# The last MLP chunk: the squared norm is applied to the hidden tiles instead of the down tiles

## The chip, the cores and the metric

The kernel runs on one core of one Trainium2 chip. What counts is the device time of one execution, in microseconds (us), as the median of several runs.

## What is computed

A two-layer block, followed by a second block of another kind, on 512 tokens of width 1024, all in float32. Only the MLP of the first block matters here; it stands at the end of each of the two layers:

```
u = rmsnorm(x, norm_mlp[l])
x = x + jnp.square(jax.nn.relu(u @ w_mlp_up[l])) @ w_mlp_down[l]
```

`rmsnorm` multiplies each token by r = 1 / sqrt(mean of squares + eps) and each column by a gain. Since r is one positive number for a token, relu(r z)^2 = r^2 relu(z)^2. The kernel computes the up product without r and applies r^2 later; `rms` holds r^2 in every partition by then. Where it is applied is free: to the hidden tile, or to the result of the down product.

## The kernel before

Tensors lie with their features in the 128 partitions and the 512 tokens along them. Every float32 product is made of three: a value is split into a high part (`a_hi`, `b_hi`, `w_hi`, written by ScalarE) and a low part (`a_lo`, `b_lo`, by VectorE; `w_lo`, by GpSimd), and TensorE adds high x high, low x high and high x low. Weights come in blocks of 1 MB: SyncE loads block n into one of two slots (L476) when the low parts of block n-2 are done, and, for some, its sums; ScalarE makes the high part (`w_split`, or `column_high` for half a block), GpSimd the low part in four pieces.

The 4096 hidden features of the MLP are worked through in 4 chunks of 8 tiles. In a chunk, four up blocks (b = 0 to 3, two tiles each) make the hidden tiles, and four down blocks add their product to the 8 tiles of x, n = 8 to 15. In chunks 1 to 3 the up blocks are computed with fewer multiplications (`fast_block` on TensorE, seven parts in four PSUM banks), for which VectorE prepares sums of weights (`weight_sums`, `sum_low`) and puts the results together (`first_sums`, `middle_sums`, `last_sums`). The orders are written out by hand for each engine; each engine runs its queue strictly in order, with semaphores between them:

- ScalarE, `fast_ups`, for each block b: the high part of one half of the next weights, the copy of the first partial product, `late_parts` (high parts of the weight sums), raw copies for the block after, then it waits for `ups_made`, takes relu of both tiles in place (L1388), and for each tile the square into `g` (L1394, signals `h_ready`) and the same square as high part into `b_hi` (L1395, signals `h_hi`). After that it goes on with block b + 1. For b = 3 the first thing is the split of the first down block (L1132).
- VectorE, `chunk`, for each block b: `weight_sums` for block b + 1, the low parts of the two hidden tiles of block b - 1 (`h_low`: `b_lo = g - b_hi`), `first_sums` (frees PSUM bank 1), `sum_low`, `middle_sums` (bank 2), `sum_low`, `last_sums` (bank 3), and it signals `ups_made`. All their element-wise instructions go through the helper `tt`, line L1689; they are told apart by their tiles.
- For each down tile n VectorE waits for TensorE and runs `x_add`: the product by `rms` in PSUM, a drain, the addition to x. In the last chunk it then signals `x_ready`; ScalarE takes x's high part and square for the next layer, VectorE the low part and the running sums of squares (`squares`, L1768).
- At the end of layer 1 TensorE begins the second block with `plain_pair`; before its fourth step it sums the squares over the partitions (`entry_sums`, L846, 16 matmuls of one column), and waits for VectorE's sums first.

Of the kernel before, what the change touches and what calls it, by code (L numbers as in the profile page):

```python
# [8 lines left out]
ALU = mybir.AluOpType  # L9
ACT = mybir.ActivationFunctionType  # L10
# [15 lines left out]
CHUNKS = 4  # L26
# [36 lines left out]
UP = 4  # L63
# [84 lines left out]
def two_blocks(nc, weights, ada, c_rows, consts, rope, tri_bias, mult_bias, tri_mask, layer_params, params, x_in, selectors, out):  # L148
    with ExitStack() as ctx:
# [92 lines left out]
        def sem(name):  # L242
            return ctx.enter_context(nc.semaphore(name))
# [116 lines left out]
        stored = sem("stored")  # L360
        ups_made = sem("ups_made")
        relu_made = sem("relu_made")
        t_near = sem("t_near")
        t_used = sem("t_used")
        t_raw = sem("t_raw")
# [762 lines left out]
        def _(act):  # L1128
# [167 lines left out]
            for L in range(LAYERS):  # L1296
# [70 lines left out]
                def fast_ups(c):  # L1367

                    at = B_MLP + 8 * c
                    for b in range(UP):  # L1370
                        k_ = UP * (c - 1) + b
                        if b + 1 < UP:
                            column_high(at + b + 1, 0).then_inc(w_hi_ready, 1)
                        else:
                            w_split(L, at + UP)
                        if k_ == 0:
                            act.wait_ge(t_split, nth(L, 4, 3))
                        p1_copy_out(L, MLP, k_)
                        if b + 1 < UP:
                            late_parts(L, MLP, k_ + 1, at + b + 1)  # L1380
                        act.wait_ge(tile_done, nth(L, LAYER_TILES, c * 16 + first_tile(B_MLP) + 2 * b + 1))
                        if b == 0:
                            ada_load_at(c, 1)
                        if b + 2 < UP:
                            raw_copies(L, k_ + 2, at + b + 2)
                        act.wait_ge(ups_made, fast_nth(L, k_, 1, 1))
                        for u in range(2):
                            nc.scalar.activation(result[MLP][u], result[MLP][u], ACT.Relu, scale=(1.0, -1.0)[u])  # L1388
                        act.drain()
                        for u in range(2):  # L1390
                            m = 2 * b + u
                            if b > 0:
                                act.wait_ge(h_split, nth(L, 8 * CHUNKS, c * 8 + m - 2))
                            nc.scalar.activation(g[:, 6 + u, :], result[MLP][u], ACT.Square).then_inc(h_ready, 1)  # L1394
                            nc.scalar.activation(b_hi[:, m, :], result[MLP][u], ACT.Square).then_inc(h_hi, 1)  # L1395
                        if b == UP - 1:
                            w_split(L, at + UP + 1)

# [288 lines left out]
        def _(dve):  # L1687
# [315 lines left out]
            with dve.Fori(0, LAYERS) as L:  # L2003
# [39 lines left out]
                def chunk(c):  # L2043
# [25 lines left out]
                    def h_low(n):  # L2069
# [2 lines left out]
                        tt(b_lo[:, n, :], g[:, 6 + n % 2, :], f32(b_hi[:, n, :]), ALU.subtract).then_inc(h_split, 1)  # L2072
                        dve.drain()

                    def t_forms(n):

                        t1, t2, t3, t4 = (m[:, n, :] for m in x_sums_f32[MLP])
                        near, far = g[:, n % 2, :], ps[4 + n % 2]
                        dve.wait_ge(t_near, nth(L, HK, n))
                        tt(t1, near[:, 0:HS], near[:, HS:S], ALU.subtract)  # L2080
                        dve.drain()
                        nc.vector.scalar_tensor_tensor(t2, far[:, HS:S], -1.0, t1, ALU.mult, ALU.subtract)
                        tt(t3, far[:, HS:S], near[:, HS:S], ALU.subtract)
                        dve.drain()
                        nc.vector.scalar_tensor_tensor(t4, far[:, 0:HS], -1.0, t2, ALU.mult, ALU.subtract
                                                       ).then_inc(t_used, 1)
                        if n == HK - 1:
                            dve.drain().then_inc(t_raw, 4)
# [18 lines left out]
                    else:  # L2107
                        for b in range(UP):
                            k_ = UP * (c - 1) + b
                            more = b + 1 < UP  # L2110
                            if more:
                                weight_sums(L, MLP, k_ + 1, at + b + 1)
                            if b > 0:
                                for u in range(2):
                                    h_low(2 * b - 2 + u)
                            first_sums(L, MLP, k_)
                            if more:
                                sum_low(L, MLP, k_ + 1, 1)
                            middle_sums(L, MLP, k_)
                            if more:  # L2120
                                sum_low(L, MLP, k_ + 1, 2)
                            last_sums(L, MLP, first + 2 * b)
                            dve.drain().then_inc(ups_made, 1)
                        for u in range(2):
                            h_low(2 * UP - 2 + u)
                    if last_chunk:
                        modulation_gain(0)
                        dve.drain()
# [5 lines left out]
                    for n in range(8, 16):  # L2134
                        if last_chunk and n == 15:
                            squares(L, n - 9, 2 * KT + n - 9, True)
                        dve.wait_ge(tile_done, nth(L, LAYER_TILES, first + n))
                        x_add(n, n - 8, last_chunk, True)
                        if last_chunk and 8 < n < 15:
                            low_next(n - 9)  # L2140
                        if last_chunk and n == 15:
# [499 lines left out]
```

## Time and profile before

| | before |
|---|---|
| median of 3 runs (lowest, highest) | 2045.96 us (2044.22, 2046.25) |
| the profiled execution, its time | 2045.99 us |
| its span, first to last instruction | 2044.1 us |
| busy in the span: TensorE | 2034.3 us (100%) |
| VectorE | 1228.3 us (60%) |
| ScalarE | 886.3 us (43%) |
| GpSimd | 1025.8 us (50%) |
| mean granted clock of TensorE | 0.999 |

The profile names engines PE (TensorE), DVE (VectorE), ACT (ScalarE), POOL (GpSimd) and SP (SyncE). A row of the timeline gives the start in us, the length in us, engine, line, operation, written tile <- read tiles, and in brackets the idle time of the engine before it with what ended it. Instructions of one engine overlap a little, so the step between two starts is shorter than their length. The last chunk of layer 0 lies at 625 to 709 us: the up blocks start at 625.4, 635.5, 645.6 and 655.6, the down tiles at 665.7. The last chunk of layer 1 lies 702.05 us later, with the same rows.

### The profile page before, as it was taken

Reading aid. Unit: us, or ns where it says so; the run is one execution under the profiler, and the core shown is the slowest. Engines: PE = TensorE matmul, PEld = TensorE weight load, DVE = VectorE, ACT = ScalarE, POOL = GpSimd, SP = SyncE. Lnnn points to the kernel's source line nnn. Section 1 sums busy time; section 2 is a strip of 40 time slices with the busy share of each in tenths; the row PEclk is TensorE's granted clock in tenths of the full one; section 3 lists DMA queues with packets and bytes.
Section 4 is the critical chain, followed back from the end, with each engine's and each line's share of the span. In section 5 each row is a group of like instructions: output and inputs, shape, how many; then the busy total and the mean of one; then the engine's idle time right before and its main releaser. Section 6 shows DMA issues by size and latency. Waiting matters only on the chain.

```text
span 2044.1 us, 29815 instructions
## 1 busy us (share of the span) xinstructions
PE 2034.3 (100%) x10920; PEld 1715.2 (84%) x10920; DVE 1228.3 (60%) x2166; ACT 886.3 (43%) x1353; POOL 1025.8 (50%) x761
## 2 busy tenths in 40 slices
PE   9999999999999999999999999999999999999999
PEld 7788778889889878877788899898877777889898
DVE  5677335576757737854356767668445478737363
ACT  4124353536345422244445455364356544535352
POOL 5454334576555554443355765554343334556555
PEclk9999999999999999999999999999999999999999
DMA  6222212343443232221233443422222112222223
GB/s 215 98 98 89 83 63 102 115 165 107 183 151 118 104 118 97 103 83 69 77 114 124 146 148 143 170 97 103 98 83 78 67 42 96 91 103 104 104 103 104
DMA packets 36083, 222.60 MB, mean 109 GB/s; under 512 B 5308, under 2 KB 5692, under 8 KB 10336
## 3 DMA queue, kind: packets, MB, share of 16 engines
q1 hardware_dynamic: 28608, 190.66, 26.5%
q10 hardware_dynamic: 7328, 30.00, 4.3%
q8 instruction: 91, 1.49, 0.3%
q14 instruction: 56, 0.46, 0.1%
HBM read 215.65 MB, written 2.10 MB: 107 GB/s over the span
## 4 chain that ended last, share of the span: by engine, by line
PE 95%; DVE 3%; DVEq 1%; issue 0%; ACT 0%; DMA 0%; ACTq 0%; POOL 0%
PE ps L554 18%; PE ps L556 17%; PE ps L555 17%; PE ps L718 6%; PE ps L720 6%; PE ps L719 6%; PE ps L571 3%; PE ps L572 3%; PE ps L573 3%; PE ps L634 2%; PE ps L603 1%; PE ps L605 1%; PE ps L604 1%; PE ps L655 1%; PE ps L644 1%
## 5 line engine op out<-in xcount | busy, mean ns | idle before, releaser
L487 POOL TENSOR_TENSOR w_lo<-w_raw,w_hi 128x512 fp32r<-128x512 f32 x544 | 737.6, 1387 | 800.6 <-ACT w_hi L1132 790.8
L1132 ACT ACTIVATE w_hi<-w_raw 128x2048 fp32r<-128x2048 f32 x134 | 256.1, 1911 | 388.9 <-PE ps L556 289.4
L554 PE MATMUL ps<-a_hi,w_hi 128*128 128x512 f32 (+1 forms) x888 | 351.8, 396 | 0.0
L556 PE MATMUL ps<-a_hi,w_lo 128*128 128x512 f32 (+1 forms) x888 | 346.2, 390 | 0.0
L555 PE MATMUL ps<-a_lo,w_hi 128*128 128x512 f32 (+1 forms) x888 | 345.8, 389 | 0.0
L501 POOL TENSOR_TENSOR w_lo<-w_raw,w_hi 128x512 fp32r<-128x512 f32 x164 | 214.8, 1333 | 166.4 <-ACT w_hi L1266 166.4
L554 PE MATMUL ps<-b_hi,w_hi 128*128 128x512 f32 x612 | 238.1, 389 | 0.0
L555 PE MATMUL ps<-b_lo,w_hi 128*128 128x512 f32 x612 | 238.1, 389 | 0.0
L556 PE MATMUL ps<-b_hi,w_lo 128*128 128x512 f32 x612 | 238.1, 389 | 0.0
L554 PEld LDWEIGHTS ps<-a_hi,w_hi 128*128 128x128 f32 (+1 forms) x888 | 165.3, 186 | 47.6 <-issue 10.5
L556 PEld LDWEIGHTS ps<-a_hi,w_lo 128*128 128x128 f32 (+1 forms) x888 | 165.2, 186 | 36.9
L555 PEld LDWEIGHTS ps<-a_lo,w_hi 128*128 128x128 f32 (+1 forms) x888 | 165.4, 186 | 34.5
L555 PEld LDWEIGHTS ps<-b_lo,w_hi 128*128 128x128 f32 x612 | 114.9, 188 | 23.9
L556 PEld LDWEIGHTS ps<-b_hi,w_lo 128*128 128x128 f32 x612 | 114.9, 188 | 23.8
L554 PEld LDWEIGHTS ps<-b_hi,w_hi 128*128 128x128 f32 x612 | 114.9, 188 | 23.8
L718 PE MATMUL ps<-a_hi,w_hi 128*128 128x256 f32 x424 | 120.2, 284 | 1.3 <-POOL w_lo L501 0.6
L720 PE MATMUL ps<-a_hi,w_lo 128*128 128x256 f32 x424 | 120.0, 283 | 0.0
L719 PE MATMUL ps<-a_lo,w_hi 128*128 128x256 f32 x424 | 120.0, 283 | 0.0
L1266 ACT ACTIVATE w_hi<-w_raw 128x1024 fp32r<-128x1024 f32 x82 | 85.7, 1052 | 61.0 <-DVE w_raw L1689 27.0
L1689 DVE TENSOR_TENSOR g<-ps,g 128x512 f32<-128x512 f32 (+1 forms) x116 | 73.4, 633 | 42.3 <-ACT g L1409 16.6
L1689 DVE TENSOR_TENSOR b_lo<-g,b_hi 128x512 fp32r<-128x512 f32 x86 | 62.6, 729 | 52.3 <-ACT b_hi L1395 36.2
L1804 DVE CUSTOM_DVE_ANT_0 pr<-ps,bias 128x512 f32<-128x512 f32 (+3 forms) x48 | 21.5, 486 | 113.8 <-issue 113.8
(391 smaller groups left out, 4520.8 us busy)
## 6 DMA issues: line engine op xcount, KB each, us to landing
w_raw<-in_weights SPq DMA_DIRECT2D x176, 1024.0 KB, 4.9
v<-in_ada ACTq DMA_DIRECT2D x24, 1024.0 KB, 4.8
out<-x SPq DMA_DIRECT2D x8, 256.0 KB, 2.0
x<-in_x_in SPq DMA_DIRECT2D x3, 512.0 KB, 7.0
w_raw<-in_weights SPq DMA_DIRECT2D x4, 256.0 KB, 5.7
yc<-in_c_rows ACTq DMA_DIRECT2D x2, 512.0 KB, 3.2
bias<-in_mult_bias ACTq DMA_DIRECT2D x1, 640.0 KB
x<-in_x_in SPq DMA_DIRECT2D x2, 256.0 KB, 4.8
```

What stands on the lines that cost most here:

```text
L487: nc.gpsimd.tensor_tensor(w_lo[:, s, piece], w_raw[:, s, piece], f32(w_hi[:, s, piece]), ALU.subtract).then_inc(w_lo_ready, 1)
L501: nc.gpsimd.tensor_tensor(quad(w_lo, s, u, kh), quad(w_raw, s, u, kh), f32(quad(w_hi, s, u, kh)), ALU.subtract).then_inc(w_lo_ready, 1)
L554: nc.tensor.matmul(o, wh, hi(kt), start=kt == 0, stop=False)
L555: nc.tensor.matmul(o, wh, lo(kt), start=False, stop=False)
L556: last = nc.tensor.matmul(o, wl, hi(kt), start=False, stop=kt == depth - 1)
L571: nc.tensor.matmul(o[u], wh, src[0][:, kt, :], start=kt == 0, stop=False)
L718: nc.tensor.matmul(o, fh[:, kt, :], mh[:, kt, :], start=kt == 0, stop=False)
L719: nc.tensor.matmul(o, fh[:, kt, :], ml[:, kt, :], start=False, stop=False)
L720: last = nc.tensor.matmul(o, fl[:, kt, :], mh[:, kt, :], start=False, stop=kt == HK - 1)
L1132: nc.scalar.activation(w_hi[:, n % 2, :], w_raw[:, n % 2, :], ACT.Copy).then_inc(w_hi_ready, 1)
L1266: return nc.scalar.activation(hi, raw, ACT.Copy)
L1689: return nc.vector.tensor_tensor(out_, a, b_, op)
```

## The change

In the last chunk (c = 3) of each layer, ScalarE only writes the two squares into `g` and signals a new semaphore, `sq_made`. VectorE multiplies each by `rms` in place (`hidden_scaled`) and signals `h_ready`; then ScalarE takes the high part from `g` by a copy (`h_high`), and VectorE the low part as before. In VectorE's queue `hidden_scaled(b - 1)` stands before `weight_sums` of block b, and for the last two tiles before their low parts. The eight down tiles of this chunk are added to x without the product by `rms`. The other chunks are as before.

```diff
@@ ScalarE, fast_ups
                             if b > 0:
                                 act.wait_ge(h_split, nth(L, 8 * CHUNKS, c * 8 + m - 2))
+                            if c == CHUNKS - 1:
+                                nc.scalar.activation(g[:, 6 + u, :], result[MLP][u], ACT.Square).then_inc(sq_made, 1)
+                                continue
                             nc.scalar.activation(g[:, 6 + u, :], result[MLP][u], ACT.Square).then_inc(h_ready, 1)
                             nc.scalar.activation(b_hi[:, m, :], result[MLP][u], ACT.Square).then_inc(h_hi, 1)
+                        if c == CHUNKS - 1:
+                            for u in range(2):
+                                h_high(c, 2 * b + u)
                         if b == UP - 1:
                             w_split(L, at + UP + 1)
@@ VectorE, chunk
+                    def hidden_scaled(b):
+
+                        for u in range(2):
+                            dve.wait_ge(sq_made, nth(L, 2 * UP, 2 * b + u))
+                            tt(g[:, 6 + u, :], g[:, 6 + u, :], rms[:, :], ALU.mult).then_inc(h_ready, 1)
+
+                    def hidden_low(b):
+
+                        for u in range(2):
+                            h_low(2 * b + u)
@@
                             more = b + 1 < UP
+                            if last_chunk and b > 0:
+                                hidden_scaled(b - 1)
                             if more:
                                 weight_sums(L, MLP, k_ + 1, at + b + 1)
                             if b > 0:
-                                for u in range(2):
-                                    h_low(2 * b - 2 + u)
+                                hidden_low(b - 1)
                             first_sums(L, MLP, k_)
@@
-                        for u in range(2):
-                            h_low(2 * UP - 2 + u)
+                        if last_chunk:
+                            hidden_scaled(UP - 1)
+                        hidden_low(UP - 1)
@@
                         dve.wait_ge(tile_done, nth(L, LAYER_TILES, first + n))
-                        x_add(n, n - 8, last_chunk, True)
+                        x_add(n, n - 8, last_chunk, not last_chunk)
```

## Rows read from the trace of the kernel before

**Rows 1.** The page: busy time of TensorE, and the weight loads (KB, us to landing).

```profile
PE 2034.3 (100%) x10920; PEld 1715.2 (84%) x10920; DVE 1228.3 (60%) x2166; ACT 886.3 (43%) x1353; POOL 1025.8 (50%) x761
...
w_raw<-in_weights SPq DMA_DIRECT2D x176, 1024.0 KB, 4.9
```

**Rows 2.** Waits of TensorE: waiter <- releaser, us in total, times, longest.

```profile
PE ps L846 <- DVE yc L1768: 0.6, 1, 0.6
```

**Rows 3.** Timeline of TensorE, layer 0: first matmul of tiles 8 and 9, and of tile 10.

```profile
665.72 0.40 PE L571 MATMUL ps<-b_hi,w_hi 128*128 128x512 f32 x1
...
676.63 0.39 PE L554 MATMUL ps<-b_hi,w_hi 128*128 128x512 f32 x1
```

**Rows 4.** Timeline of VectorE in the up blocks of the last chunk, layer 0.

```profile
635.68 0.69 DVE L1689 TENSOR_TENSOR g<-ps,g 128x512 f32<-128x512 f32 x1
636.84 0.69 DVE L1689 TENSOR_TENSOR bias<-ps,w_raw 128x512 f32<-128x512 f32 x1 [0.46 <-ACT ps L1261]
...
639.62 0.68 DVE L1689 TENSOR_TENSOR b_lo<-g,b_hi 128x512 fp32r<-128x512 f32 x1
640.53 0.69 DVE L1689 TENSOR_TENSOR b_lo<-g,b_hi 128x512 fp32r<-128x512 f32 x1 [0.23 <-issue]
...
643.04 0.69 DVE L1689 TENSOR_TENSOR ws_m<-ps,ws_m 128x512 fp32r<-128x512 f32 x1 [0.87 <-ACT ws_m L1279]
643.65 1.18 DVE L1689 TENSOR_TENSOR g<-ps,g 128x512 f32<-128x512 f32 x2
...
645.76 0.69 DVE L1689 TENSOR_TENSOR g<-ps,g 128x512 f32<-128x512 f32 x1
...
655.84 0.69 DVE L1689 TENSOR_TENSOR g<-ps,g 128x512 f32<-128x512 f32 x1
```

**Rows 5.** Timeline of ScalarE in the same blocks.

```profile
636.74 1.14 ACT L1388 ACTIVATE g<-g 128x512 f32<-128x512 f32 x2
637.95 0.63 ACT L1394 ACTIVATE g<-g 128x512 f32<-128x512 f32 x1
638.49 0.61 ACT L1395 ACTIVATE b_hi<-g 128x512 fp32r<-128x512 f32 x1
...
640.05 1.04 ACT L1266 ACTIVATE w_hi<-w_raw 128x1024 fp32r<-128x1024 f32 x1
...
656.67 1.15 ACT L1388 ACTIVATE g<-g 128x512 f32<-128x512 f32 x2 [1.61 <-DVEq L2123]
...
660.00 1.90 ACT L1132 ACTIVATE w_hi<-w_raw 128x2048 fp32r<-128x2048 f32 x1
```

**Rows 6.** Timeline of GpSimd in the same blocks: low pieces of the weights.

```profile
641.17 2.56 POOL L501 TENSOR_TENSOR w_lo<-w_raw,w_hi 128x512 fp32r<-128x512 f32 x2 [4.20 <-ACT w_hi L1266]
...
661.97 5.04 POOL L487 TENSOR_TENSOR w_lo<-w_raw,w_hi 128x512 fp32r<-128x512 f32 x4 [4.42 <-ACT w_hi L1132]
```

**Rows 7.** Timelines of GpSimd and VectorE where they run together (387 and 1387 us).

```profile
386.72 6.38 POOL L487 TENSOR_TENSOR w_lo<-w_raw,w_hi 128x512 fp32r<-128x512 f32 x4 [9.12 <-ACT w_hi L1132]
...
387.26 1.30 DVE L1689 TENSOR_TENSOR b_lo<-g,b_hi 128x512 fp32r<-128x512 f32 x1 [1.14 <-ACT b_hi L1350]
...
1387.53 1.61 DVE L1689 TENSOR_TENSOR yc<-yc,g 128x512 f32<-128x512 f32 x1
```

**Rows 8.** Timelines of VectorE and TensorE at the end of layer 1.

```profile
1412.28 0.69 DVE L1689 TENSOR_TENSOR ps<-ps,rms 128x512 f32<-128x512 f32 x1
1413.05 0.69 DVE L1689 TENSOR_TENSOR x<-x,ps 128x512 f32<-128x512 f32 x1
...
1416.20 1.05 PE L846 MATMUL ps<-kc,yc 128*128 128x1 f32 x8 [0.64 <-DVE yc L1768]
```

**Rows 9.** Stretches: us, busy (x instructions) by engine, TensorE's granted clock, DMA share, GB/s.

```profile
1418.00:1423.00 5.00, 5.00 (x17) 3.95 (x17) 3.92 (x11) 0.74 (x4) 4.15 (x4) 0.66 0.01 3
1441.00:1443.00 2.00, 2.00 (x18) 1.98 (x17) 2.00 (x4) 1.14 (x3) 1.78 (x2) 1.00 0.00 0
1652.00:1656.00 4.00, 1.71 (x14) 1.28 (x13) 3.99 (x4) 1.81 (x12) 4.00 (x3) 1.00 0.00 0
```

More of the change, by code:

```diff
@@ L362, in two_blocks @@
         relu_made = sem("relu_made")
+        sq_made = sem("sq_made")
         t_near = sem("t_near")
```

## The prediction, made before the change was run

> **What bounds the kernel now.** I read the page's busy times first: TensorE is busy for practically the whole span [rows 1]. So the change can only matter where it makes TensorE wait, or takes a wait away. Second, the waits of TensorE: the one that the change touches is 0.6 us, before the column sums at the end of the second layer [rows 2]. Third, the timelines of the last MLP chunk of layer 0, engine by engine. TensorE goes from the four up blocks into the first down tile at 665.72 without a gap [rows 3]; an up block takes 10.08 us there, the distance at which rows of VectorE and ScalarE repeat (645.76 and 655.84 are two `last_sums`) [rows 4]. The question for every other engine is by how much it is ahead of that beat.
>
> The two engines that matter alternate. VectorE ends block b with `last_sums` and signals `ups_made`; only then ScalarE does two relus, two squares and two high parts [rows 5]. Before, VectorE uses this time for `weight_sums` of the next block (from 636.84), and takes the low parts afterwards, when ScalarE's results are there (639.62, 640.53) [rows 4]. The order on VectorE is what hides ScalarE.
>
> **What the change does to that order.** `hidden_scaled(b-1)` stands ahead of `weight_sums`. It waits for ScalarE's squares, which wait for `ups_made`. Everything behind it on VectorE waits too: the weight sums, the low parts, `first_sums` (which frees PSUM bank 1) and the next `ups_made`. ScalarE in turn waits for the product before its high parts, and behind these stands the split of the next weights, for which GpSimd waits, and behind GpSimd SyncE's load. So I add up one round of the loop, from the start S of one `last_sums` to the start of the next:
> - to the first relu 0.83 (655.84 to 656.67), to the first square 1.21 (636.74 to 637.95), the square 0.63, handing over to VectorE 0.14 (from the end of `last_sums`, 656.53, to 656.67) [rows 4, 5]. The first product starts at S + 2.81.
> - Two products at the step of 0.61 (643.04 to 643.65): the weight sums start at S + 4.03. They take 2.78 (636.84 to 639.62), the low parts 0.91 each (639.62 to 640.53), `first_sums` with its drain 0.77 (taken from 1412.28 to 1413.05), one low sum 0.61, and the two middle sums and the second low sum 2.11 (643.65 to 645.76) [rows 4, 8]. Sum: 12.12, against a beat of 10.08.
> - In the first round ScalarE comes 0.23 later (relu at 636.74, not at 635.68 + 0.83), because it still copies raw weights [rows 4, 5].
>
> **GpSimd on top.** Before, both low parts run while GpSimd is idle: it starts again at 641.17, after 4.20 idle [rows 6]. `b_lo<-g,b_hi` reads two SBUF tiles, and when such an instruction meets one of GpSimd's it waits until that one is over: at 387.26, 0.54 us into a GpSimd piece of about 1.25, it takes 1.30 instead of 0.69, and the sums of `yc` take 1.61 [rows 7]. In the new order ScalarE starts the column split at S + 4.77 (second product's end 4.11, 0.14, high part 0.52), takes 1.04, and GpSimd works from S + 5.9. The low parts want to start at S + 6.81: the first waits 0.34 for the end of the first piece, the second about 1.0. That is 1.35 a round, so a round is 13.5, the first 13.7. The products themselves (`g` and `rms`, also both in SBUF) fall in GpSimd's idle time.
>
> The Trainium skill, SBUF — State Buffer, section Who interferes with whom, says that a VectorE instruction with two SBUF inputs and a GpSimd instruction that reads SBUF exclude each other, and that the one that started first keeps the port for its whole length. Were both low parts of a round to meet a whole piece, that rule would allow 2.5 us a round instead of 1.35 and a stall of 7.5 us a layer instead of the 5.2 below; the trace agrees with the rule's form, but the low part that I show took 1.30, not 1.9.
>
> **The stall.** `last_sums` of block 0 starts at 635.68 [rows 4]; of block 1 at 649.4 (before 645.76), of block 2 at 662.9 (before 655.84). From there: high parts begun, split of the first down block's weights at S + 4.77, 1.90 long, 0.07 to GpSimd, 1.26 for its first piece: 670.9. Before, this was 661.97 + 1.26 = 663.2, that is 2.5 us before TensorE needs it at 665.72 [rows 3, 5, 6]. So TensorE starts the down tiles 5.2 us late. It loses them in three places: about 0.9 before block 3 (its weights' low piece comes at 656.5, not before 655.64), 2.0 at its second part (`first_sums` of block 2 ends at S + 10.7 = 660.1 with bank 1), and 2.3 at the first down tile. Once there it waits no more: the last low part is needed 7 steps of 1.36 (two tiles in 10.91 us, 8 steps) after 670.9, at 680.4; `last_sums` of block 3 starts near 672.2 (behind ScalarE's split and its copy of the first partial product), and that low part ends 6.0 later, at 678.2. The weight load behind GpSimd starts when all four pieces of the down block are done, 674.8, and lands 4.9 later [rows 1]; it is needed near 682. Both layers alike: **+10.4 us**.
>
> Bounds: if the low parts meet nothing, a round is 12.12 and the stall 2.5 a layer. If each takes 1.61 as at 1387.53 [rows 7], a round is 0.5 longer, and the stall 6.2. I take 5.2, since the low parts stand right on GpSimd's two pieces.
>
> **What it gives.** In the down tiles 8 products a layer go, 0.77 each with the drain (1412.28 to 1413.05), 12.3 us of VectorE in all. Seven of eight are hidden: a down tile takes 5.45 us on TensorE [rows 3], and it waits for VectorE in none of them, nor at the start of layer 1. At the end of layer 1 the last tile's product heads the chain product, add, square on ScalarE, sums on VectorE, and TensorE waits 0.64 for it [rows 2, 8]. 0.77 less takes the wait away: -0.64. And the clock: behind this wait and the 16 one-column matmuls that follow it, the granted clock over 1418 to 1423 is 0.66, down to the 1.2 GHz level for part of it; 0.34 x 5 us = 1.7 us lost. After 16 such small matmuls without a wait (1441 to 1443) it stays at 1.00 [rows 9]. I take the 1.7 as given back; the other end is 0.
>
> **Sum.** The profiled execution took 2045.99 us (span 2044.1, 1.9 around it), the median is 2045.96, so both are the same base. 2045.99 + 10.4 - 0.64 - 1.7 = **2054.1 us**.
>
> **Rivals.**
> 1. *The low parts meet no GpSimd work* (GpSimd's pieces run earlier or later than I place them). 2.5 a layer: 2045.99 + 5.0 - 2.3 = 2048.7. For it: before, all 0.69. Against: the column split is due just ahead of them in the same chain.
> 2. *The slack holds* (the other side). GpSimd's low piece is 2.5 us ahead at the downs, and VectorE has idle times between its instructions in a block (0.46, 0.23 and 0.87 us) [rows 4]. If two rounds together lose no more than 2.5, TensorE never waits and only the end of layer 1 counts: 2045.99 - 2.3 = 2043.7. The point: a round of 11.3 or less. It needs the wait for the squares to be filled by something; nothing in the queue behind it can overtake it.
> 3. *More than summed.* Low parts as long as the `yc` sums, 6.2 a layer; and the clock falls behind the stall at the first down tile. A wait of about 2.3 after full work is in no row: 2.29 idle within 1652 to 1656 left the clock at 1.00, 0.64 with one-column work lowered it for 1.7 us [rows 9]. With 1.7 a layer: 2045.99 + 12.4 + 3.4 - 0.64 = 2061.2.
>
> **Chances.** Forecast (4.5 to 6.2 a layer, 2052 to 2056.5) 0.50; rival 1 0.20; rival 2 0.12; rival 3 or values towards it 0.15; faster by more than I can name a cause for 0.03. What can be told from no change is about 0.2%, 4.1 us: rivals 1 and 2 fall within it. Slower 0.50 + 0.15 + 0.03 (the upper part of rival 1's spread) = 0.68, same 0.29, faster 0.03. The range takes in rivals 1 and 3 and leaves out rival 2: 2048.2 to 2061.3.
>
> **What would show it.** In the changed kernel's trace: in both last chunks a product at about S + 2.8 on VectorE with an idle of over 2 us before it, ended by ScalarE; `last_sums` 13.5 us apart instead of 10.08; low parts of over 0.9 us in blocks 1 and 2; TensorE waits in block 3 and at the first down tile, 5 us together, ended by GpSimd's `w_lo` or VectorE; ScalarE's split of the first down block near 667.7 instead of 660.00; no wait before the column sums and clock 1.00 behind them. The prediction is wrong if VectorE's rounds stay at 10.08 (rival 2), or if the low parts stay at 0.69 (rival 1), or if the clock still falls at the end of layer 1 (1.7 more).

## The result, and the profile after

The changed kernel takes 2048.52 us (2047.98 to 2049.59, 20 executions) against 2045.80 us (2043.90 to 2046.98, 20 executions) for the kernel before: a ratio of 1.0015, 95% interval 1.0009 to 1.0021. That is slower by 2.7 us. I had forecast 2054.1, 8.1 more than before, so the sign and the mechanism came out, and the size did not. The profiled execution took 2048.59 (span 2046.6), 2.6 us more than that of before, so the two traces can be read against each other.

The page and TensorE's longest waits, where [rows 1, 2] stood (columns of the waits: us in total, times, longest):

```profile
PE 2033.4 (99%) x10920; PEld 1715.1 (84%) x10920; DVE 1228.2 (60%) x2166; ACT 887.9 (43%) x1353; POOL 1028.9 (50%) x761
...
PE ps L719 <- DVE g L1696: 3.0, 2, 1.5
PE ps L572 <- POOL w_lo L488: 2.8, 2, 1.4
```

Each of the two waits comes once per layer, and no wait before the column sums (L847 in this kernel) is left. Timeline of TensorE, layer 0 and the end of layer 1, answering to [rows 3, 8]:

```profile
658.78 0.38 PE L719 MATMUL ps<-a_hi,w_hi 128*128 128x256 f32 x1 [1.47 <-DVE g L1696]
...
669.08 0.49 PE L572 MATMUL ps<-b_hi,w_hi 128*128 128x512 f32 x1 [1.41 <-POOL w_lo L488]
...
1422.42 0.95 PE L847 MATMUL ps<-kc,yc 128*128 128x1 f32 x8
```

TensorE stands at two places: in up block 3, for the bank that `first_sums` of block 2 frees, and at the first down tile, for its weights' low part. The down tiles start at 669.08 instead of 665.72 [rows 3]. Timeline of VectorE in the same stretch, answering to [rows 4]:

```profile
635.75 0.69 DVE L1696 TENSOR_TENSOR g<-ps,g 128x512 f32<-128x512 f32 x1
638.68 1.29 DVE L1696 TENSOR_TENSOR g<-g,rms 128x512 f32<-128x512 f32 x2 [2.23 <-ACT g L1396]
...
648.60 0.68 DVE L1696 TENSOR_TENSOR g<-ps,g 128x512 f32<-128x512 f32 x1
651.25 1.29 DVE L1696 TENSOR_TENSOR g<-g,rms 128x512 f32<-128x512 f32 x2 [1.97 <-ACT g L1396]
652.46 0.68 DVE L1696 TENSOR_TENSOR bias<-ps,w_raw 128x512 f32<-128x512 f32 x1
...
655.24 0.84 DVE L1696 TENSOR_TENSOR b_lo<-g,b_hi 128x512 fp32r<-128x512 f32 x1
656.31 1.47 DVE L1696 TENSOR_TENSOR b_lo<-g,b_hi 128x512 fp32r<-128x512 f32 x1 [0.23 <-issue]
657.96 0.69 DVE L1696 TENSOR_TENSOR g<-ps,g 128x512 f32<-128x512 f32 x1 [0.18 <-issue]
658.86 0.69 DVE L1696 TENSOR_TENSOR ws_m<-ps,ws_m 128x512 fp32r<-128x512 f32 x1 [0.21 <-issue]
659.47 1.18 DVE L1696 TENSOR_TENSOR g<-ps,g 128x512 f32<-128x512 f32 x2
...
661.17 0.68 DVE L1696 TENSOR_TENSOR g<-ps,g 128x512 f32<-128x512 f32 x1
```

`last_sums` stand at 635.75, 648.60 and 661.17: rounds of 12.85 and 12.57 us, against 10.08 before. In front of each pair of products VectorE is idle for about 2 us, and ScalarE's square ends it. Timelines of ScalarE and GpSimd, answering to [rows 5, 6]:

```profile
661.99 1.15 ACT L1389 ACTIVATE g<-g 128x512 f32<-128x512 f32 x2 [4.90 <-DVEq L2142]
...
665.74 1.90 ACT L1133 ACTIVATE w_hi<-w_raw 128x2048 fp32r<-128x2048 f32 x1
...
654.23 3.00 POOL L502 TENSOR_TENSOR w_lo<-w_raw,w_hi 128x512 fp32r<-128x512 f32 x2 [5.35 <-ACT w_hi L1267]
...
667.71 5.02 POOL L488 TENSOR_TENSOR w_lo<-w_raw,w_hi 128x512 fp32r<-128x512 f32 x4 [6.31 <-ACT w_hi L1133]
```

The split of the first down block starts at 665.74, where it started at 660.00, and its first low piece is done near 669.0, when TensorE starts.

Setting each TensorE matmul of the two traces side by side gives the account of the 2.6 us. TensorE is later by 6.9 at the end of layer 1: 3.4 in each last chunk, and 0.2 at the start of layer 1 (709 us), where two executions of one kernel also differ by some tenths. It gains 0.9 at the column sums, where the wait is gone. It gains 1.6 just behind them, where the granted clock is now 1.00 and was 0.66 [rows 9]. The column sums stand 6 us later here, so the same code lies at 1424 to 1429 (view of stretches, same columns):

```profile
1424.00:1429.00 5.00, 5.00 (x27) 4.19 (x27) 3.16 (x12) 0.24 (x2) 3.50 (x3) 1.00 0.15 25
```

And it gains 2.4 at L1046 (L1045 before; 1653 to 1655 us there), in code that the change does not touch. At 1665 (1667.72 in the changed kernel) it gives 0.5 of that back in a wait that the trace puts down to nothing. Together that is 2.0 us, called the loss at L1045 from here on. I had no term for this. The timelines of the kernel before there, TensorE, GpSimd and VectorE:

```profile
1653.74 0.66 PE L1045 MATMUL ps<-kc,k 128*128 128x128 f32 x4 [1.27 <-DVE k L1689]
1655.41 0.66 PE L1045 MATMUL ps<-kc,k 128*128 128x128 f32 x4 [1.02 <-DVE k L1689]
...
1650.65 5.85 POOL L487 TENSOR_TENSOR w_lo<-w_raw,w_hi 128x512 fp32r<-128x512 f32 x4 [27.48 <-ACT w_hi L1132]
...
1650.66 1.27 DVE L1689 TENSOR_TENSOR mcol<-mcol 128x8 f32<-128x8 f32 x1 [0.40 <-issue]
1652.01 3.35 DVE L1689 TENSOR_TENSOR k<-g,mcol 128x512 f32<-128x512 f32 x2
```

and in the changed kernel VectorE, GpSimd and, further on, TensorE:

```profile
1654.84 0.17 DVE L1696 TENSOR_TENSOR mcol<-mcol 128x8 f32<-128x8 f32 x1
1655.08 2.37 DVE L1696 TENSOR_TENSOR k<-g,mcol 128x512 f32<-128x512 f32 x2
...
1655.15 5.95 POOL L488 TENSOR_TENSOR w_lo<-w_raw,w_hi 128x512 fp32r<-128x512 f32 x4 [27.48 <-ACT w_hi L1133]
...
1667.72 0.47 PE L572 MATMUL ps<-a_hi,w_hi 128*128 128x512 f32 x1 [0.50 <-issue]
```

Before, VectorE stands still for 0.40 us in front of a product of 128x8 values, with nothing to wait for that the profile shows. GpSimd's pieces start 0.01 us ahead of it. The small product then takes 1.27 us instead of 0.17, the two `k` products 3.35 instead of 2.37, and TensorE waits 1.27 + 1.02. After, the standstill is not there, and the first `k` product starts 0.07 us ahead of GpSimd's pieces instead of behind the first of them.

The sum: +6.9 - 0.9 - 1.6 - 2.0 = +2.4, against 2.6 measured between the two profiled executions; rounding and the first microseconds make the rest.

### The profile page after: what moved, and what is told of

Its sections match the earlier page's. It is cut to its first block, busy times and chain, and to the rows that moved or that the text cites. A ratio compares the mean times of both kernels' runs of the same rounds, so it can differ in the third digit from the quotient of the medians.

```text
span 2046.6 us, 29799 instructions
## 1 busy us (share of the span) xinstructions
PE 2033.4 (99%) x10920; PEld 1715.1 (84%) x10920; DVE 1228.2 (60%) x2166; ACT 887.9 (43%) x1353; POOL 1028.9 (50%) x761
## 4 chain that ended last, share of the span: by engine, by line
PE 92%; DVE 3%; DVEq 2%; ACT 1%; issue 1%; ACTq 1%; DMA 0%; POOL 0%
PE ps L555 18%; PE ps L557 17%; PE ps L556 17%; PE ps L719 5%; PE ps L721 5%; PE ps L720 5%; PE ps L572 3%; PE ps L573 3%; PE ps L574 3%; PE ps L635 1%; PE ps L604 1%; PE ps L606 1%; PE ps L605 1%; PE ps L656 1%; PE ps L645 1%
## 5 line engine op out<-in xcount | busy, mean ns | idle before, releaser
L719 PE MATMUL ps<-a_hi,w_hi 128*128 128x256 f32 x424 | 120.5, 284 | 4.2 <-DVE g L1696 3.0
L1696 DVE TENSOR_TENSOR x<-x,ps 128x512 f32<-128x512 f32 x80 | 55.0, 688 | 60.0 <-PE ps L557 45.7
```

What stands on the lines that cost most here:

```text
L719: nc.tensor.matmul(o, fh[:, kt, :], mh[:, kt, :], start=kt == 0, stop=False)
L1696: return nc.vector.tensor_tensor(out_, a, b_, op)
```

## The experiments

Two theories stood against each other for the stall. Theory 1: it is the wait for ScalarE's squares at the head of VectorE's queue, with GpSimd's contention on top. The rival: it is the added work of VectorE, wherever it stands. For the 3.6 us at the end of layer 1 and at L1045, the question was which part of them belongs to the change.

**Both kernels again** (no edit), for a second profile of each.

> The kernel before, unchanged, for a second profile. In the first profile TensorE lost 0.64 us before the column sums at the end of layer 1, the clock fell behind it (1.7 us), and in the second block VectorE's small product of `mcol` met GpSimd's first piece of `w_lo` at 1650.66 (1.27 us instead of 0.17), which cost TensorE 2.3 us at L1045; with the change these 2.3 became 0.3. Theory 1 (who comes first at 1650 is chance, and differs between executions of one kernel): about one profile in two shows a wait at L1045 of 0.3 instead of 2.3, with a time near 2044.0. Theory 2 (the order at 1650 follows from where the kernel's layout puts the two, and the change moved it): L1045 shows 2.3 us again and the time is near 2046. The wait at L846 and the clock are there in both.

Measured 2044.33, span 2042.3. TensorE's row at the column sums and the stretch behind them:

```profile
1416.11 1.05 PE L846 MATMUL ps<-kc,yc 128*128 128x1 f32 x8 [0.64 <-DVE yc L1768]
...
1418.00:1423.00 5.00, 5.00 (x28) 4.20 (x27) 4.23 (x12) 0.64 (x4) 4.11 (x4) 1.00 0.01 3
```

The wait is the same 0.64 as in [rows 8], yet the clock stayed at 1.00, and this execution is 1.66 shorter. The loss at L1045 is back in full (1.28 and 3.35 for the same two rows, 2.3 of waits). So the first differs from execution to execution of one program, and the second is in both profiles of it.

> The changed kernel once more, for a second profile. Theory 1: as in the first, waits of TensorE of 1.5 and 1.4 us in each last chunk, no wait before the column sums of layer 1, granted clock 1.00 behind them, at most 0.3 us at the later transposes; time 2048.5. Rival (the clock falls behind the column sums by chance here too, as in one of two profiles of the kernel before): clock below 0.8 over these 5 us and 2050.

Measured 2048.32, span 2046.4, clock 1.00, with the same waits of 3.0 and 2.8.

The mean granted clock of every execution sorts the times of before: the 67 executions taken beside the timed experiments have 30 at 1.000 with medians of 2044.3 to 2044.4, and 37 at 0.999 or less: 30 near 2046.0, and 7 at 0.998 or 0.997 with 2046.9 to 2048.8, of which none was profiled. The changed kernel is at 1.000 in all 21. So the change does give the 1.7 back, but only to those executions that had lost it.

**The down tiles alone.** The squared norm is left out of the last chunk's part of x altogether.

```diff
-                        x_add(n, n - 8, last_chunk, True)
+                        x_add(n, n - 8, last_chunk, not last_chunk)
```

> The kernel before with only the second half of the change: in the last chunk the down tiles are added without the product by `rms`, and nothing else takes its place (so the squared norm is left out of this chunk's result). Theory 1: the wait at L846 (0.6 us) goes and the clock stays at 1.00 behind it, nothing else moves: 2.5 us less than before in the part up to 1500 us. Rival (the clock falls anyway behind the 16 one-column matmuls, with or without a wait): 0.7 to 0.9 less. Rival (VectorE's 12 us less in the down tiles frees nothing): no change.

Measured 2041.74 (2041.60 to 2041.96), ratio 0.9982 (0.9973 to 0.9991), clock 1.000 in all 11 executions. No wait is left at L846 and none at L1045. Against before at the same clock (2044.36, 8 executions) it is faster by 2.6 us. Its trace divides this: TensorE gains 0.9 at the column sums and 2.4 at L1045, and a wait of 0.8 a little later (L571, for `x`) takes as much back, 2.5 in all. Up to the column sums nothing moves by more than 0.1, so the products that are gone from the other seven down tiles had cost TensorE nothing.

**The hidden tiles alone.** The change's new order, with the down tiles' product kept, so the last chunk's part of x has the squared norm twice.

```diff
-                        x_add(n, n - 8, last_chunk, not last_chunk)
+                        x_add(n, n - 8, last_chunk, True)
```

> The changed kernel with the product by `rms` kept in the down tiles of the last chunk (so this chunk is scaled twice): only the first half of the change. Theory 1: the two last chunks lose 3.5 us each in TensorE's waits (1.5 at the second part of block 3, 1.4 to 1.9 at the first down tile), and the wait and the low clock at the end of layer 1 are there again: about 2.5 us more than the changed kernel, 7.0 more than before up to the end of layer 1, a time near 2051 to 2052.8. Rival (the two halves work on each other: with less VectorE work in the down tiles the up blocks of the same chunk can't gain, but the end of layer 1 can lose its wait through the later start): the same time as the changed kernel, 2048.5.

Measured 2050.35 (2049.04 to 2050.75), ratio 1.0022 (1.0012 to 1.0031). The waits at L719 and L572 are those of the changed kernel (3.0 and 2.8). The wait at the column sums is back (0.64), and so are the two levels: 7 executions at 0.999 with a median of 2050.43, 4 at 1.000 with 2049.38. At a clock of 1.000 it is 5.0 above before (2044.36), at 0.999 it is 4.5 above it (2045.97): +6.8 for the two stalls, -2.0 at L1045, where `k` takes 2.37, and a few tenths at 709 us that differ between executions. That is below the 2051 to 2052.8 that I expected, since the loss at L1045 did not come back with the down tiles' products. The whole stall lies in the new order, and none of it in the down tiles.

**The products behind the weight sums.** The same work of the change, every product included, in another order on VectorE.

```diff
-                            if last_chunk and b > 0:
-                                hidden_scaled(b - 1)
                             if more:
                                 weight_sums(L, MLP, k_ + 1, at + b + 1)
+                            if last_chunk and b > 0:
+                                hidden_scaled(b - 1)
                             if b > 0:
                                 hidden_low(b - 1)
```

> The changed kernel with one pair of calls exchanged on VectorE: `hidden_scaled(b - 1)` stands behind `weight_sums` of block b, not ahead of it. Theory 1 (VectorE's wait for ScalarE's squares, 2.2 us a round, is what makes a round 12.6 to 12.9 us instead of 10.08): the weight sums fill that wait again, a round is at most 11, the split of the first down block's weights comes about 662 instead of 665.7, TensorE waits 0 to 0.5 us a layer instead of 3.5; the time is 5 to 7 us below the changed kernel, 2042 to 2043.5. Rival (it is the 1.2 us of products and GpSimd's port that make the round, not the wait): a gain of at most 2 us, 2046.5 to 2048.5.

Measured 2041.61 (2041.18 to 2042.60), ratio 0.9982 (0.9973 to 0.9991), clock 1.000 in all 11: faster than both kernels. Timelines of VectorE and ScalarE:

```profile
635.59 0.69 DVE L1696 TENSOR_TENSOR g<-ps,g 128x512 f32<-128x512 f32 x1
...
639.52 1.28 DVE L1696 TENSOR_TENSOR g<-g,rms 128x512 f32<-128x512 f32 x2
640.97 0.69 DVE L1696 TENSOR_TENSOR b_lo<-g,b_hi 128x512 fp32r<-128x512 f32 x1 [0.17 <-ACT b_hi L1351]
641.90 0.69 DVE L1696 TENSOR_TENSOR b_lo<-g,b_hi 128x512 fp32r<-128x512 f32 x1 [0.24 <-issue]
...
646.67 0.68 DVE L1696 TENSOR_TENSOR g<-ps,g 128x512 f32<-128x512 f32 x1
...
657.57 0.68 DVE L1696 TENSOR_TENSOR g<-ps,g 128x512 f32<-128x512 f32 x1
...
662.15 1.90 ACT L1133 ACTIVATE w_hi<-w_raw 128x2048 fp32r<-128x2048 f32 x1
```

No idle time stands before the first two pairs of products, all low parts take 0.69, and the rounds are 11.08 and 10.90. The split of the first down block starts 2.2 later than before instead of 5.7. That is inside the 2.5 us by which it was ahead, and TensorE waits for nothing in the last chunk. This settles theory 1 against the rival: the same added work costs 6.9 us at one place of the queue and nothing at another, where the kernel is as fast as the one without any of the products (2041.74).

**Relu and the squared norm in one operation on VectorE.** The product is put ahead of the squares instead of behind them, so ScalarE is never waited for in the middle of a round. ScalarE's relus go in the last chunk; `rms` holds r there, and the other chunks' down tiles take its square from `mt`.

```diff
+                            if last_chunk:
+                                dve.drain()
+                                for u in range(2):
+                                    nc.vector.scalar_tensor_tensor(result[MLP][u], result[MLP][u], 0.0, rms[:, :],
+                                                                   (ALU.max, ALU.min)[u], ALU.mult)
                             dve.drain().then_inc(ups_made, 1)
...
-                        x_add(n, n - 8, last_chunk, True)
+                        x_add(n, n - 8, last_chunk, not last_chunk)
```

> The kernel before, in whose last chunk VectorE takes relu and the norm in one operation right after `last_sums` (max or min with zero, times r, in place; `rms` keeps r and a free tile holds its square for the chunks before), ScalarE drops its relus and squares twice as before, and the down tiles are added without a product. Nobody waits for anybody new. Theory 1: VectorE's round is at most 11 us and the slack of 2.5 us at the first down tile is enough, TensorE does not wait in the last chunk; the end of layer 1 as with the down tiles alone: 2041.6, the same as with the products behind the weight sums. Rival (the two operations stand ahead of `ups_made` and of the weight sums, meet GpSimd's last pieces of the round and make rounds of over 11.3 us): TensorE waits at the first down tile, 1 us or more a layer, 2043.5 or more.

Measured 2043.45 (2043.00 to 2044.11), ratio 0.9990 (0.9981 to 0.9999), clock 1.000 in all 11. Timelines of VectorE and TensorE:

```profile
659.47 1.93 DVE L2127 SCALAR_TENSOR_TENSOR g<-g,rms 128x512 f32<-128x512 f32 x2
...
666.94 0.49 PE L571 MATMUL ps<-b_hi,w_hi 128*128 128x512 f32 x1 [0.75 <-POOL w_lo L487]
```

Rounds of 11.19 and 11.51 (`last_sums` at 635.99, 647.18, 658.69) put the split at 663.60, 3.6 later than before, and TensorE waits 0.75 a layer at the first down tile. That is the rival's time, and not the 2041.6 of theory 1. With the wait gone there is still a cost once the rounds are longer than the slack: about 0.9 a layer over the previous experiment. The pair of operations took 1.65 in the first block and 1.92 and 1.93 in the next two, where the last two of GpSimd's pieces run at the same time. Low parts met GpSimd here too: 1.48 in the first round, 1.11 behind 0.58 of idle time in the second. So this kernel is not free of contention, and how its rounds divide was not tested.

**GpSimd's pieces short.** The changed kernel, but the two first low pieces of the weights of up blocks 1 to 3 in each last chunk are a quarter as deep, so three quarters of those low parts are not renewed.

```diff
-                low_quad(s, 0, 0)
-                low_quad(s, 0, 1)
+                deep = 1 if n < LAYERS * LAYER_BLOCKS and k_ % LAYER_FAST > 2 * UP else HK
+                low_quad(s, 0, 0, deep)
+                low_quad(s, 0, 1, deep)
```

> The changed kernel, in which GpSimd makes only a quarter of each of the first two low pieces of the weights for up blocks 1 to 3 of the last chunk (the other three quarters of these low parts are left as they were from an earlier block, so this chunk's low products are not the reference's). In the changed kernel both low parts of a round meet these two pieces on the SBUF port: 0.84 and 1.47 us instead of 0.69 each, 0.93 us a round, and a round is 12.85 and 12.57 us. Theory 1 (the port adds to the round): low parts of 0.7, rounds of 11.9 and 11.6, TensorE's waits in the last chunk 1.6 us a layer instead of 3.5; time 3.7 us below the changed kernel, 2044.8. Rival (the low parts have room in the round, because something behind them waits longer anyway): low parts of 0.7 but rounds as before and 2048.5.

Measured 2044.83 (2044.47 to 2045.04), ratio 0.9997 (0.9988 to 1.0006), clock 1.000 in all 11. Timelines of GpSimd and VectorE:

```profile
653.62 0.89 POOL L503 TENSOR_TENSOR w_lo<-w_raw,w_hi 128x128 fp32r<-128x128 f32 x2 [5.35 <-ACT w_hi L1268]
...
654.61 0.68 DVE L1697 TENSOR_TENSOR b_lo<-g,b_hi 128x512 fp32r<-128x512 f32 x1
655.52 0.69 DVE L1697 TENSOR_TENSOR b_lo<-g,b_hi 128x512 fp32r<-128x512 f32 x1 [0.23 <-issue]
```

The low parts are back at 0.69, and the rounds shrink to 11.92 and 11.64 (`last_sums` at 636.05, 647.97, 659.61): exactly the 0.93 that the two low parts had over 0.69 each in the changed kernel (0.84 + 1.47 - 1.38). The stall falls from 6.9 to 3.2 us, both counted from the reordered kernel's 2041.61. Taking the contention with GpSimd away thus gives 3.7 us of the stall back; 3.2 are left for the wait for ScalarE with the two products. The two do not simply add up, since the 2.5 us a layer by which GpSimd is ahead are used up first, and in the reordered kernel the contention is gone together with the wait.

**Where VectorE stands still.** The kernel before, with eight one-column memsets in front of the second block's work on VectorE; what is computed stays the same.

```diff
+            for spare in range(8):
+                nc.vector.memset(top[:, 2, spare:spare + 1], 0.0)
             dve.wait_ge(a_turned, 1)
```

> The kernel before with eight one-column memsets (128x1, no work) more in VectorE's program in the second block, ahead of the place at L1045. In both profiles of the kernel before, VectorE stands still for 0.40 us (issue) ahead of a small product of `mcol`, meets GpSimd's first piece there and TensorE loses 2.3 us at L1045; in all four kernels whose VectorE program has another length this standstill is elsewhere and TensorE loses 0.3 us or less. Theory 1 (the standstill sits at a fixed place of VectorE's program and moves with its length): the wait at L1045 becomes 0.3, the times lie 2.0 us below those of the kernel before in both of its groups, at about 2042.3 and 2044.0. Rival (the eight products less in the down tiles or the products in the up blocks shift GpSimd against VectorE): 2.3 us at L1045 and the times of before.

Measured 2044.23 (2042.63 to 2046.21) against 2045.04 for before, ratio 0.9994 (0.9985 to 1.0003): the times alone, spread over two levels of the clock, don't tell it from no change. The profile does. Timeline of VectorE and the stretch behind the column sums:

```profile
1650.40 0.17 DVE L1689 TENSOR_TENSOR mcol<-mcol 128x8 f32<-128x8 f32 x1
1650.64 2.37 DVE L1689 TENSOR_TENSOR k<-g,mcol 128x512 f32<-128x512 f32 x2
...
1418.00:1423.00 5.00, 5.00 (x18) 3.99 (x18) 3.93 (x11) 0.83 (x4) 4.24 (x4) 0.66 0.01 3
```

The standstill is gone from the small product, `k` takes 2.37, and TensorE does not wait at L1045. The clock fell in this execution, as it does in some of before, and it still took only 2044.08. At equal mean clock the gain is 1.8 to 1.9: 2042.63 against 2044.41 at 1.000 (one execution against 16), 2044.22 against 2046.07 at 0.999 (8 against 9). Two more executions were at 0.998, at 2045.79 and 2046.21.

**The same, the other way round.** One kernel without the loss might be luck of its phase. So I took the fast one with the down tiles alone and gave VectorE its instruction count back, with almost no time.

```diff
                     if scaled:
                         tt(ps[t % 4][:, :], ps[t % 4][:, :], rms[:, :], ALU.mult)
                         dve.drain()
+                    elif scaled is None:
+                        nc.vector.memset(top[:, 2, n:n + 1], 0.0)
+                        dve.drain()
...
-                        x_add(n, n - 8, last_chunk, True)
+                        x_add(n, n - 8, last_chunk, None if last_chunk else True)
```

> The kernel downs_only (the last chunk's down tiles are added without the product by the squared norm, so the last chunk's part of x lacks that factor) with VectorE's instruction count put back: where a product and its drain went, a one-column memset of about 0.06 us and a drain stand. So VectorE has as many instructions as the kernel before at every place, but almost none of the time back. Theory A (the 0.40 us standstill of VectorE hangs on how many instructions stand ahead of it in its program, and it is what costs 2.0 us at L1045 when it lands ahead of the last small gate operation there): the standstill is back at the mcol operation near 1648.5, that operation takes 1.27, the k products 3.35, TensorE waits 2.3 at L1045, clock 1.00, no wait at L846; 2041.7 + 2.0 = 2043.7. Theory B (the loss at L1045 went because the work ahead of it got shorter or its phase against GpSimd moved by the removed 0.77 us): nothing comes back, 2041.8.

Measured 2043.88 (2042.41 to 2045.45, 10 executions), ratio 0.9992 (0.9983 to 1.0002). Theory A named 2043.7. But its profile shows only half of the loss: the standstill is back at the same operation, and the operation takes 0.17. GpSimd's and VectorE's timelines:

```profile
1648.29 5.93 POOL L487 TENSOR_TENSOR w_lo<-w_raw,w_hi 128x512 fp32r<-128x512 f32 x4 [27.49 <-ACT w_hi L1132]
...
1648.30 0.17 DVE L1689 TENSOR_TENSOR mcol<-mcol 128x8 f32<-128x8 f32 x1 [0.40 <-issue]
1648.54 3.28 DVE L1689 TENSOR_TENSOR k<-g,mcol 128x512 f32<-128x512 f32 x2
```

This execution was the shortest of the ten, so I profiled a second one.

> The kernel downs_padded again, unchanged (the last chunk's part of x lacks the factor of the squared norm), for the profile of a second execution. In the first one VectorE's standstill of 0.40 us was back at L1045's mcol, but that operation took 0.17 and the execution 2042.41, where most others took 2043.3 to 2044.0. Theory A (a race of 10 ns with GpSimd's piece decides by how much L1045 loses): where the execution takes 2043.6, mcol takes about 1.27, the k products about 3.3, and TensorE waits 2.3 in all at L1045; where it takes 2042.4, mcol takes 0.17 and the wait is 1.0 again. The standstill of 0.40 stands ahead of mcol in either. Theory B (the spread comes from elsewhere): mcol takes 0.17 and TensorE waits 1.0 whatever the time. If the granted clock is 0.999 and the time near 2045.3, a stretch with a clock below 1.00 is to be found: at 1418 to 1426, as in the kernel before, or behind L1045 (1650 to 1660), where TensorE waited.

Measured 2043.73:

```profile
1648.55 5.84 POOL L487 TENSOR_TENSOR w_lo<-w_raw,w_hi 128x512 fp32r<-128x512 f32 x4 [27.48 <-ACT w_hi L1132]
...
1648.56 1.27 DVE L1689 TENSOR_TENSOR mcol<-mcol 128x8 f32<-128x8 f32 x1 [0.40 <-issue]
1649.91 3.35 DVE L1689 TENSOR_TENSOR k<-g,mcol 128x512 f32<-128x512 f32 x2
```

Now the small product takes 1.27, and TensorE waits 2.3 at L1045 instead of 1.0. Both rows show a start 0.01 us behind GpSimd's, so what decides between 0.17 and 1.27 does not stand in them; that it is the order in which the two engines come to SBUF is argued and not shown. The standstill itself is at the same operation both times. Theory A holds in this: the place of the standstill follows the number of VectorE's instructions ahead of it, and it pushes the small product onto GpSimd's start. The changed kernel bears it out. It has no standstill at L1046, but one in front of an operation that had none before, in both of its profiles:

```profile
1425.87 0.17 DVE L1696 TENSOR_TENSOR qcol<-ps,qcol 128x8 f32<-128x8 f32 x1 [0.44 <-issue]
```

What makes VectorE stand still was not found.

Against the kernel without the loss (2041.74) the standstill costs 0.7 us where the product just gets through (2042.41) and 2.0 where it does not (2043.73).

One thing stays open. Four of the ten executions of this kernel have a mean clock of 0.999 and times of 2044.82 to 2045.45, though neither profile shows a wait at L846, and both are at 1.00 over 1412 to 1426 and 1648 to 1660. All 65 executions of the five kernels with neither that wait nor the loss at L1045 were at 1.000. Which stretch loses the clock in those four was not caught in a profile.

## Why the prediction was wrong in size

**The order on VectorE as the cause, and its places.** Right. The products wait about 2 us for ScalarE's squares, and all that was named as queued behind them came late: `first_sums` with bank 1, the split, the low piece. The sum of the stall was wrong: 3.4 a layer instead of 5.2, which is 3.5 us of the miss of 5.6. The round is where it failed. Term by term for the second round (from the rows at 648.60 to 661.17):

| term | forecast | measured |
|---|---|---|
| start of `last_sums` to first product | 2.81 | 2.65 |
| two products | 1.22 | 1.21 |
| weight sums | 2.78 | 2.78 |
| two low parts (0.91 each) with GpSimd's contention | 3.17 | 2.72 |
| `first_sums` to the low sum | 0.77 | 0.90 |
| low sum | 0.61 | 0.61 |
| middle sums and second low sum | 2.11 | 1.70 |
| sum | 13.47 | 12.57 |

Two terms carry the miss. The contention was placed right and sized too large: I let it cost 1.35, from GpSimd's start at S + 5.9. GpSimd starts at S + 5.63 (654.23 - 648.60), and the low parts lose 0.15 and 0.78. And the 2.11 was read as work, from a start to a start in [rows 4], but 0.4 of it was not. Between the two starts stands the second low sum, here before and after:

```profile
645.01 0.69 DVE L1689 TENSOR_TENSOR ws_m<-ps,ws_m 128x512 fp32r<-128x512 f32 x1 [0.18 <-ACT ws_m L1279]
...
648.00 0.68 DVE L1696 TENSOR_TENSOR ws_m<-ps,ws_m 128x512 fp32r<-128x512 f32 x1
```

Before, it was 1.36 from the middle sums to it and 0.75 from it to `last_sums`; after, 1.10 and 0.60. The first step had a wait for ScalarE's `ws_m` in it (0.18 of idle time in the row), which is gone when VectorE itself is later. What made the second step longer is not in the rows. I had charged a wait of before as if it were an instruction.

**The places of the stall.** I named three: 0.9 before block 3, 2.0 at its second part, 2.3 at the first down tile. There were two, and TensorE became later by 1.7 at each. Block 3's weights came in time, since GpSimd's first piece ran from 654.23 and not from about 655.3. The split of the first down block came at 665.74 instead of near 667.7: two rounds forecast too long by 0.9 each, and the split at S + 4.57 in its round and not at S + 4.77. The 2.5 us by which it had been ahead were right: 5.7 later, less 2.5, gives 3.2 and TensorE started 3.4 later.

**How much the contention took.** The Trainium skill, SBUF — State Buffer, section Who interferes with whom, states that the instruction that came first keeps the port for its length. Both low parts started beside a running piece and took 0.84 and 1.47, not the 1.9 of a whole piece each; the first met only a piece's last bit. GpSimd paid too: its two pieces took 3.00 us there and 2.56 before. The rule's form agrees, and its largest value (7.5 us a layer) was far off here. The small product of 128x8 values at L1045 took 1.10 us longer when it started 0.01 us behind a piece of about 1.25: that is the case in which nearly a whole piece is paid.

**Down tiles, end of layer 1 and clock.** The seven hidden products per layer cost nothing on TensorE, as forecast. The wait of 0.64 went and gave 0.9 on TensorE's shift. The clock stayed up and gave 1.6. Against one profiled execution both terms were right. But the clock is below 1.000 in only 37 of 67 executions of before, so it is a gain of the median and not of each execution. A sum made against a median that sits on one side of two levels should say so.

**The missing term.** 2.0 us at L1045 was in no step. The row of 2.29 idle between 1652 and 1656 stood in my own [rows 9]; I used it for the clock and never asked what made it. It is an interaction of two engines in code 240 us behind the change, and it went with a change in VectorE's instruction count. That the change has this effect is luck, and nothing in its idea brings it about. Without it the kernel would have come out near 2050.5. The two misses together, 3.5 and 2.0, make the 5.6 us between 2054.1 and 2048.5 but for 0.1.

**The rivals.** The slack was not there to hold in the changed kernel. Its point of decision fits the runs: two rounds may lose 2.5 together, a round of 11.3. The reordered kernel has 11.08 and 10.90 and no wait; relu on VectorE has 11.19 and 11.51 and a wait of 0.75. The first rival named 2048.7, and the kernel took 2048.5, but that is a coincidence: its condition, low parts that meet no GpSimd work, does not hold. The kernel in which it does hold was built with short pieces: it stalls 1.6 a layer, where I had 2.5, since its rounds are 11.92 and 11.64 and not 12.35 and 12.12, mostly for the same 0.4. The clock did not fall behind the new stalls of 1.5 and 1.4 us after full work: the mean is 1.000 in all 21 executions. So nothing bears out the third rival's fall of the clock.

**The direction** held for the cause that I gave: at equal clock the stall (+6.9) outweighs what the down tiles give (0.9 and 2.0).

## What to carry to other kernels

In a queue that runs strictly in order, a new operation goes behind work that needs nothing from the other engine; here the same products cost 6.9 us ahead of the weight sums and none behind them. When a round is summed from start-to-start distances, look at the idle time that stands in brackets in the rows between, since it shrinks when the engine itself is late, and the whole distance may shrink by more than the brackets say. And read every wait of the bottleneck engine in the whole trace before the sum, far from the change too: one that rests on two engines starting within 0.01 us of each other can go or come with an edit that has nothing to do with it.

## What the runs showed of the hardware that was not expected

- A standstill of 0.40 us of VectorE, released by nothing in the profile, stands at a fixed instruction of a given program: at the same operation in both profiles of before and in both of the padded kernel. It moved away when eight one-column memsets, or the change itself, altered the number of VectorE instructions ahead of it, and came back when that number was restored. In both profiles of the changed kernel it stands at another operation (0.44). What it is was not found.
- A TENSOR_TENSOR of 128x8 values in SBUF takes 0.17 us alone and 1.27 when it comes just behind the start of a GpSimd piece of about 1.25 (and 0.17 in another execution, with the same 0.01 us between the starts). The pair of 128x512 products behind it takes 2.37 when it starts 0.07 us ahead of GpSimd's pieces and 3.28 to 3.35 when the first of them had started before it; a pair that meets no piece takes 1.29 (the kernel with eight memsets, a little later):

```profile
1659.89 1.29 DVE L1689 TENSOR_TENSOR k<-g,mcol 128x512 f32<-128x512 f32 x2
```

- The same wait of 0.64 us with 16 one-column matmuls behind it left the granted clock at 1.00 in one profiled execution of the kernel before and at 0.66 over 5 us in the other; it fell too in the profiles of the hidden tiles alone and of the eight memsets. The times of before lie in two main groups 1.7 us apart, and the mean clock of an execution (1.000 or 0.999) tells them apart.
